# Splitting the normed features by halves inside the attention, with C's queries moved and four low parts taken there

## The reference

```python
lat = project_heads(h, w_in[l], ...)     # queries, keys, values of three attentions A, B, C, and gate_logits
y = mix_latent(lat, cts, a_sink[l], w_branch[l], w_out[l])
# mix: o_a, o_b, o_c = three attentions with softmax
g_a, g_b, g_c = jnp.split(jax.nn.sigmoid(gate_logits), 3, axis=-1)     # gate_logits = h @ w_in[:, 1696:]
(g_a * (o_a @ w_branch_a) + g_b * (o_b @ w_branch_b) + g_c * (o_c @ w_branch_c)) @ w_out
x = layer_norm(ALPHA * x + g1 * y, ...)
# then an expert-choice mixture of 16 SwiGLU experts of 1024 x 1024 x 3, and a second layer norm
```

## Time and profile before

| | us |
|---|---|
| median of 3 runs | 1766.28 (1763.41 to 1766.48) |
| the profiled execution | 1767.51 |
| its span, first to last instruction | 1765.7 |
| TensorE busy (matmul) | 1504.7 (85%) |
| VectorE busy | 506.8 (29%) |
| ScalarE busy | 399.5 (23%) |
| mean granted clock of TensorE | 0.916 |

### The profile page before, as it was taken

The page is one execution under the profiler, slowest core; times in us unless marked ns, Lnnn a source line. Parts: engine busy times, 40 slices in busy tenths (PEclk is TensorE's granted clock), DMA queues, the critical chain, the costliest instruction groups (busy, mean ns, idle before and its releaser), DMA issues.

```text
span 1765.7 us, 23068 instructions
## 1 busy us (share of the span) xinstructions
PE 1504.7 (85%) x9748; PEld 814.8 (46%) x9748; DVE 506.8 (29%) x1002; ACT 399.5 (23%) x856; POOL 23.3 (1%) x47
## 2 busy tenths in 40 slices
PE   7999998999988998899888798989976676676764
PEld 3543446888874343433222274568752333332322
DVE  0225576433552000011010454765630000000003
ACT  1213677222231010200000132864320001000000
POOL 1000000000000000000000100000000000000000
PEclk9999999999988999999999899999977768776767
DMA  9645921333557999999999921046989999999995
GB/s 365 243 180 242 384 83 63 111 90 101 191 218 286 421 421 421 421 421 420 422 421 422 327 84 48 1 142 196 358 326 421 421 421 421 420 421 420 421 421 225
DMA packets 101509, 522.69 MB, mean 296 GB/s; under 512 B 11024, under 2 KB 13344, under 8 KB 47136
## 3 DMA queue, kind: packets, MB, share of 16 engines
q1 hardware_dynamic: 97712, 509.97, 72.5%
q0 software_dynamic: 3392, 10.85, 1.8%
q10 hardware_dynamic: 304, 0.40, 0.1%
HBM read 520.04 MB, written 1.15 MB: 295 GB/s over the span
## 4 chain that ended last, share of the span: by engine, by line
PE 55%; SPq 23%; DMA 12%; DVE 6%; ACT 2%; issue 1%; DVEq 0%; ACTq 0%
PE psum L527 51%; SPq L1093 23%; DMA ring<-in_w_down 7%; PE psum L607 4%; DMA ring<-in_w_up 3%; DMA A<-in_w_down 2%; DMA ring<-in_w_ada 1%; ACT hT L1239 1%; DVE small L1706 1%; DVE PR L1725 1%; DVE X L1736 1%; DVE X L1737 1%; DVE X L1843 1%; DVE small L1711 0%; DVE stats L1849 0%
## 5 line engine op out<-in xcount | busy, mean ns | idle before, releaser
L527 PE MATMUL psum<-ring,A 128*32 128x256 f32 (+1 forms) x1920 | 278.6, 548 | 72.8 <-DMA ring<-in_w_up 40.6
L527 PE MATMUL psum<-ring_r,h_hi 128*128 128x512 f32 x704 | 218.2, 391 | 6.9 <-DVE h_lo L1743 5.8
L527 PE MATMUL psum<-A 128*32 128x256 f32 (+5 forms) x1152 | 185.4, 540 | 38.5 <-DMA A<-in_w_up 19.3
L527 PEld LDWEIGHTS psum<-ring,A 128*32 128x32 f32 (+1 forms) x1920 | 88.6, 137 | 249.0 <-issue 104.4
L1877 DVE TENSOR_TENSOR W<-W,psum 128x512 f32<-128x512 f32 (+1 forms) x32 | 17.7, 555 | 548.5 <-PE psum L527 548.5
L527 PE MATMUL psum<-ring,PR 128*32 128x256 f32 (+1 forms) x1080 | 143.4, 498 | 29.2 <-DMA ring<-in_w_down 29.1
L527 PE MATMUL psum<-ring,hT 128*128 128x512 f32 (+3 forms) x512 | 165.1, 476 | 3.0 <-DVEq L1497 1.2
L527 PE MATMUL psum<-ring_r,h_lo 128*128 128x512 f32 x384 | 149.7, 390 | 0.0
L527 PEld LDWEIGHTS psum<-ring_r,h_hi 128*128 128x128 f32 x704 | 132.1, 189 | 35.2 <-issue 6.6
L527 PEld LDWEIGHTS psum<-A 128*32 128x32 f32 (+3 forms) x1152 | 61.5, 143 | 126.2 <-issue 58.4
L527 PEld LDWEIGHTS psum<-ring,hT 128*128 128x128 f32 x512 | 85.7, 194 | 68.8 <-issue 66.6
(11 more groups left out here) (201 smaller groups left out, 1415.6 us busy)
## 6 DMA issues: line engine op xcount, KB each, us to landing
ring<-in_w_down SPq DMA_DIRECT2D x93, 1024.0 KB, 25.9
ring<-in_w_up SPq DMA_DIRECT2D x85, 1024.0 KB, 25.3
ring<-in_w_gate SPq DMA_DIRECT2D x80, 1024.0 KB, 25.3
ring<-in_w_ada SPq DMA_DIRECT2D x40, 1024.0 KB, 9.0
A<-in_w_up SPq DMA_DIRECT2D x40, 1024.0 KB, 26.0
A<-in_w_gate SPq DMA_DIRECT2D x38, 1024.0 KB, 26.4
ring<-in_w_in SPq DMA_DIRECT2D x36, 1024.0 KB, 5.1
A<-in_w_down SPq DMA_DIRECT2D x28, 1024.0 KB, 26.0
```

What stands on the lines that cost most here:

```text
L527: return nc.tensor.matmul(o, a, b, start=start, stop=stop, skip_group_check=True)
```

## The change

- The features are split in two entries, by halves of the slices k, each over all tiles of the layer (`split_features`): 4 x 512 = 2048 elements in layer 0, 4 x 256 = 1024 in layer 1. The list now begins: features half 0, gate weights half 0, gate weights half 1, features half 1, branch weights, outputs by tile.
- The queries of C move from 3072 to 1536 in A, which leaves 4096 to 6144 free in the attention.
- Four high parts are made in the latent attention, at i = 8, 22, 25 and 28, and their four low parts there too, each on VectorE at the end of the step after (i = 9, 23, 26, 29), behind max(i) and mult(i-1).
- The gate products of slice-half h wait for entry h of the features rather than for the tile's.

```diff
-EARLY_SPLITS = 2
-EARLY_SPLITS_AT = (24, 28)
+EARLY_SPLITS = 4
+EARLY_SPLITS_AT = (8, 22, 25, 28)
...
-        qT = {"A": part(A, 0, 3, 512), "C": part(A, 3072, 3, 512), "B": part(A, 6144, 4, 512)}
+        qT = {"A": part(A, 0, 3, 512), "C": part(A, 1536, 3, 512), "B": part(A, 6144, 4, 512)}
...
-            return 2 * len(tiles(l)) + 3
+            return EARLY_SPLITS + 1 + len(tiles(l))
...
+            def split_features(l, h):
+
+                ks, cols = slice(4 * h, 4 * h + 4), slice(P * tiles(l)[0], 512)
+                hi = h_hi[:, ks, cols]
+                splits[l].append((hT[:, ks, cols], hi, h_lo[:, ks, cols], hi.bitcast(F32), None))
+                return len(splits[l])
...
+                        h_split[0] = split_features(l, 0)
                         wg = gate_pieces(n, br)
-                        for t in ts:
-                            h_split[t] = split_rows(l, hT, h_hi, h_lo, t)
+                        h_split[1] = split_features(l, 1)
...
-                            need(h_split[t])
+                            need(h_split[h])
...
+                    if s == 1 and i - 1 in EARLY_SPLITS_AT:
+                        low(l, EARLY_SPLITS_AT.index(i - 1))
                 return step
...
-                for i in range(EARLY_SPLITS):
-                    low(l, i)
```

## The result

The changed kernel takes 1775.94 us (median of 5 runs, 1771.31 to 1776.71) against 1766.48 (5 runs, 1763.41 to 1768.24): a ratio of 1.0041 with a 95% interval of 1.0027 to 1.0055, or 7.2 us slower (4.8 to 9.7). The two medians by themselves lie 9.5 apart, inside that interval; the ratio is what the text goes by. Its profiled execution took 1776.71, with a span of 1774.9.

The account below looks back on a forecast made before the run. TensorE bounds the kernel, busy 85% of the span; other engines count only where it waits. 12.9 us added in the attention less 5.78 removed: 7.1 slower, 1766.3 + 7.1 = 1773.4 us, range 1766.5 to 1779.3.

Parts of the forecast that it names:

- The term for the clock: TensorE's new gaps in the attention: longest 2.5 us, shorter than a 2.89 gap that kept the clock, so nothing added.
- The gap goes: Before the gates: first gate product follows O(7) at once, removing 2.89 us in each layer, 5.8 together.
- Moved queries, new order: C's queries, list order and `need` by halves: no instruction or DMA more or less; zero.
- The walk: Attention, step by step: layer 0 adds 1.13 and 6.51 us, layer 1 0.68 and 4.58; sum 12.9.
- turn-taking: Attention: low(i) stands ahead of max(i+2) on VectorE, so exp(i+2) waits for high part, then low part.
- The walk for the high parts alone: Attention, if low parts hid wholly: O(7) 2.3 us late in layer 0, 0.9 in layer 1.
- The sign in VectorE's waits: Sign of being right: VectorE's wait for ScalarE, `L1743 <- ACT L1381`, of 1 to 2 us four times per attention.
- The clock: Rival: clock falls in new 1.7 to 2.5 us attention gaps, both layers; 7.1 + 8 slower, 1781 us; chance 0.06.
- one of my signs of being wrong: Attention: a granted clock below 1.00 in the stretches with TensorE's new gaps.
- my price of 4 us for each: Clock fall in a layer's attention: some 8 us of products at half speed, costing 4 us.
- 0.71, 0.06 and 0.05: Chances for slower by over 0.2%: forecast's share, clock falling in new gaps (1781), gates still waiting for something else (1779.2).

Follow-up runs that it names:

- The second trace: The changed kernel run once more, unaltered, for one more trace: 1777.99 us (one run).
- the first two experiments: Changed kernel with its four low parts on VectorE after the attention, then instead each two steps later inside it: ratios 0.9975 and 0.9979 against the kernel before.
- the one-pair run: Against the free-steps version: high part 0 at i = 8 and its low part at the end of step 9; 1753.92 us (one run).
- the first experiment: Changed kernel with its four low parts on VectorE after the attention, high parts still at i = 8, 22, 25, 28: ratio 0.9975 against the kernel before.
- the weights moved: Kernel before with its two high parts at i = 13 and 15 instead of 24 and 28: ratio 0.9987.
- the free steps: Changed kernel with high parts at i = 9, 13, 15, 34 and low parts after the attention: 1753.85 us, ratio 0.9925 against the kernel before.
- the features alone: Free-steps version with gate weights' high parts back at i = 24 and 28, features at 13 and 34: ratio 0.9951 against the kernel before.

## Why the prediction was right

The measured time fell in the range, and the account of the waits held to a few tenths of a microsecond. The term for the clock, put at nothing, did not hold; it is answered under 4 and 5.

1. *The gap goes, 5.8 us.* Shown: the gap is 2.9 in all four traces of kernels that split the features by tile after the attention and 0 in all others. The term was too small as a price, though: see 4 and 5.
2. *Moved queries, new order: zero.* Shown, 0.9998.
3. *The walk, 12.9 us added.* Layer 0: 73.8 less 64.5 is 9.3; O(6) at half clock is 1.4 of it (3.35 less 1.95), which leaves 7.9 against 7.64. The single steps held too: O(4) waits 2.01 (1.80 more than the old 0.25 was the walk's number), O(5) 2.48 (2.5), and max(10) follows the first low part as costed, 2.21 behind its start (2.20). Layer 1: 7.2, of which O(5) at half clock made 1.7, leaves 5.5 against 5.26. The second trace agrees: 9.5 less 1.7 is 7.8 in layer 0, and 6.9 less 1.4 for O(5) and 0.3, by which the slow O(4) put O(5) off, is 5.2 in layer 1. That the larger part is turn-taking, and not the amount of work, is shown by the first two experiments, and its price for one pair by the one-pair run. The walk for the high parts alone was somewhat too dear: it said 2.3 and 0.9, and the first experiment shows 1.8 and 0.6. The sign in VectorE's waits, four of 1 to 2 us in each attention, came less exactly: 1.48, 1.39, 1.59 and 2.22 in layer 0, and 0.46, 1.38, 1.59 and 3.10 in layer 1, the last behind the slow O(5).
4. *The clock.* I gave it 0.06 and argued from the 2.89 us gap, after which the earlier trace rows show the full clock. A granted clock below 1.00 in these stretches was one of my signs of being wrong, and it came in all four attentions of the changed kernel. The reading was wrong: one trace was taken for a rule. Of the eight such gaps in four traces five were followed by the lower level (both of the kernel with only the queries moved, both with the weights moved, one of two in the second trace of the kernel before), and of the fourteen gates' starts without a gap, in seven traces, none. The change paid 1.4 us in layer 0 and 1.7 in layer 1 for a fall inside the attention, and my price of 4 us for each was too high: the low level held for 3.5 us in layer 0 and 7 us in layer 1, and of what ran in it only one product O was long and on the chain of waits.
5. *The total.* 7.1 forecast, 7.2 measured, partly by luck. The two stages alone grew by 10.6: the walk's part by 13.4 (for 12.9), the falls inside the attention by 3.1 that were in no term of my sum, less 5.9 for the gaps. What works against it is that the falls behind the two gaps, which went, had cost the kernel before something in some executions. Their price can be read. From layer 0's first gate product to the output projection's first products (chain of waits) eight traces without a fall there took 177.2 to 177.3 us, among them the kernel before, 462.25 less 285.02. The two with a fall took 178.8, among them the kernel with moved queries, 464.15 less 285.35. So a fall of 3.5 us cost 1.6:

```profile
462.25 5.73 PE psum L527 x24
```

```profile
464.15 5.70 PE psum L527 x24
```

In layer 1, from the first gate product to the output projection's first transposes, traces without a fall took 88.9, the two with 3.5 us of it 90.3 and 90.5, and the one with 7 us 91.7. The five falls together cost 9.0 us in four traces, 2.2 us for an execution on average; that mean is an estimate from few traces. With it the change comes to 10.6 less 2.2, 8.4 slower, inside the measured 4.8 to 9.7.

A slip in the chances: slower by more than 0.2% adds up to 0.71, 0.06 and 0.05, which is 0.82 and not 0.81. Nothing else hangs on it.

The same estimate goes far to explain why the free steps gained 13.3 rather than 9.3: 9.3 and 2.2 is 11.5, inside the 11.0 to 15.4. For the features alone it gives 5.9 and 2.2, 8.1, where 8.7 (5.3 to 12.0) was measured. The first two experiments come to 5.7 and 4.8 faster, against 4.4 (2.5 to 6.2) and 3.7 (1.6 to 6.0). The intervals are too wide to show that nothing else has a part in it.

The Trainium skill, "TensorE: Matmul & The Clock Gate", section "What's actually happening", says that the measure behind the clock gate runs freely, independent of the kernel, so that the place of a transition differs from run to run. The traces agree: in layer 1 the changed kernel's clock fell at O(5) in one trace and at O(4) and O(5) in the other, and behind layer 1's gap of 2.89 us the kernel before kept its full clock in one trace and not in the other.

## What to carry to other kernels

Look for work that is handed from one engine to another inside a loop which the same two engines already share. If the second half stands right behind the first in the queues, it holds the loop back for up to the sum of both durations (here 4.1 us for a pair of 2048 elements); what the loop's slack does not hide is lost, 7.9 us for four pairs in layer 0. Put the second half a few steps later, or behind the loop, and most of that goes (here 11 us in the whole kernel for the same instructions). Choose the step by the engine's own idle time in the trace, not by what is ready there: with two or four high parts at steps where ScalarE waited, layer 0's attention took the same 62.6 us, and with two at i = 24 and 28 it took 64.5. And read a gap in TensorE's stream as possibly dearer than its length.

## What the runs showed of the hardware

- After a gap of 2.9 us in front of dense TensorE work the clock was at its lower level in five of eight cases, four times for 3.5 us at a price of 1.4 to 1.6 us, and once for 7 us at a price of 2.8. With no gap at the same place it was so in none of fourteen.
- In the attention of the changed kernel, whose gaps from O(4) to O(7) are 0.3 to 2.5 us long, the clock fell in four attentions of four, for 3.5 or 7 us. In one of them it fell right behind the first long gap, of 2.02 us; the same gap was followed by the full clock in seven other attentions. One trace that shows no fall behind a gap does not show that there will be none.
